# In the expert gather, gelu and weighing take two picks at a time, all but the last four

## The chip, the cores and the metric

The kernel runs on one core of a Trainium2 chip. The metric is the device time of one execution in microseconds (us), the median of several runs.

## The reference, cut to what matters

Two transformer blocks on 256 tokens of 1024 channels, in float32. The last part of the second block is a feed-forward layer that looks up single-neuron experts: for every token and each of 8 heads, 16 of 16384 experts are picked by product keys, and each pick costs one row `u` and one row `v` of 1024 numbers.

```
q = x @ w_query; s = q . sub_keys          # per head, two sides of 128 keys
top 16 per side -> 256 sums -> top 16      # best_s, idx
g = softmax(best_s)                        # 16 weights per head
act = gelu(x . u[idx])                     # one dot product per pick
y = sum over picks of g * act * v[idx]
out = x + y
```

## The kernel before

Everything ahead of the lookup (projections, convolution, attention, the recurrent branch) takes the first 590 us and is untouched. The rest is the gather stage. The tokens are two tiles (`t`) of 128, one token on each partition. A "pick" `g` is one expert slot of one tile: 16 (head, tile) pairs of 16 picks, 256 picks in all. For each pick GpSimd (POOL) starts one indirect DMA (`gather`, L2434) that fetches for each of the 128 tokens its own row of 2048 numbers (`u` and `v` side by side, 8 KB), 1.05 MB in all. For the last two picks (`HALVED`) `u` and `v` come by separate half-size gathers (L2443), all `u` before all `v`.

The rows land in a ring of nine buffers, `UV` (in the profile's names `conv_in`, `big`, `row`, `work_two`). Gather `g` waits until the buffer of pick `g - 9` is free.

Each pick then passes four engines' queues, each of them in order:

- VectorE (DVE): `dot_product(g)` multiplies the `u` half with the normed tokens and sums it up to one number per token (L2062).
- ScalarE (ACT): `spread_value(g)` takes the gelu of that number (L1293). It then waits for the weighing and writes a 128x128 diagonal matrix with the weighed numbers into one of twelve places (L1299).
- VectorE: `weigh(g)` multiplies the gelu with the softmax weight and the inverse of the softmax sum (L2072). It stands behind `dot_product(g + 1)` in VectorE's queue (only in the last picks ahead of it).
- TensorE (PE): `add_value(g)` multiplies the diagonal with the `v` half and adds it up in PSUM, two halves of 512 columns, four matmul records a pick (L779). Its end frees the buffer.

The last pick of all (`LAST`, 255) has no diagonal: `last_value` (L2080) adds it on VectorE, and `add_values` (L2091) then adds the sums from PSUM in two halves, each of which is sent out by a DMA of its own.

Beside this, spread over the picks by hand, the next heads are chosen: `choose` on VectorE (L1961 to L2054) in small steps, one after each pick; `choose_exp` on ScalarE with two loads of its function table (L898) at the picks of `exp_at`, all of them odd numbers. In each quarter of 64 picks the next queries are projected: a weight piece is split into two parts (`hi` on ScalarE, L907, at the first and eighteenth pick; `lo` on VectorE), PE does one group of matmuls after each add of picks 4 to 17 and 22 to 35, ScalarE copies the queries (L1275) at pick 36 of the quarter, PE scores them (L765) at pick 37, ScalarE copies the scores (L1264) at pick 38, and `choose` starts on them. The order inside each engine's queue is the order of the loop over `g`:

```
for g in range(ALL_PICKS):        # DVE
    if g < LAST and g != LAST - 3:
        dot_product(g + 1)
    weigh(g)
    if g == LAST - 3:
        dot_product(g + 1)
    ...                           # one step of choose, lo
```

Of the kernel before, what the change touches and what calls it, by code (L numbers as in the profile page):

```python
# [11 lines left out]
ALU = mybir.AluOpType  # L12
ACT = mybir.ActivationFunctionType
# [27 lines left out]
PEER_TOPK = 16  # L41
# [21 lines left out]
class Marks:  # L63
# [13 lines left out]
    def mark(self, kind, key=None, *others, by=1):  # L77

        value = self.values[kind] = self.values.get(kind, 0) + by
        for name in (("#" + kind, value), (kind, key), *others):  # L80
            self.names[name] = kind, value
        return self.sem(kind), by
# [108 lines left out]
def build(nc, known, x, mem, vectors, weights, rg_w_a, rg_w_x, norm_ffn, sub_keys_t, experts,  # L191
          out):
    with ExitStack() as ctx:
        def sb(name, shape, dt=F32, space=ctx):
            return space.enter_context(nc.sbuf_tensor(name, [P, *shape], dt))

        def psum(name, n):
# [3 lines left out]
        mark, now, at = marks.mark, marks.now, marks.at  # L201
# [13 lines left out]
        probs = Ring("probs", [sb(f"probs{i}", [2, 384]) for i in range(2)])  # L215
        probs_t = Ring("probs_t", [early_small[:, 640 + i * 512:1152 + i * 512] for i in range(2)])
        ident, ones, ones64, later = (sb(n, [P]) for n in (
            "ident", "ones", "ones64", "later"))
# [24 lines left out]
        def tiles4(ap):  # L243
            return ap.rearrange("p (j t) -> p j t", j=4)
# [83 lines left out]
        weight = [sel[:, 256 + t * 128:256 + (t + 1) * 128] for t in range(TT)]  # L328
        dot = [sel[:, 512 + t * 128:512 + (t + 1) * 128] for t in range(TT)]
        coef = dot  # L330
# [42 lines left out]
        for p in range(PIECES_ALL):  # L373
# [15 lines left out]
        diag_places = [probs.buffers[i % 2][:, i // 2 % 2, i // 4 * P:(i // 4 + 1) * P]  # L389
                       for i in range(12)]  # L390
        heads = [(t, h) for i in range(4) for t in range(TT) for h in (2 * i, 2 * i + 1)]
        picks = [(t, h * PEER_TOPK + j) for t, h in heads for j in range(PEER_TOPK)]
# [6 lines left out]
        HALVED = (ALL_PICKS - 2, ALL_PICKS - 1)  # L399
        LAST = ALL_PICKS - 1  # L400
        final_sum = {t: max(g for g in range(LAST) if picks[g][0] == t) for t in range(TT)}
        half_rows = experts.rearrange("n (h d) -> (n h) d", h=2)
        queries, queries_free = tiles4(work_one[:, :]), ("work free", work.holder[1])

# [3 lines left out]
        def under(g):  # L408

            i = g // GROUP + 1  # L410
            return (i, g % GROUP) if i < 4 else (None, None)
# [480 lines left out]
        def act(e):  # L892
            W = Reached(at)
            held = [None]

            def table(*sets):
                if held[0] not in sets:
                    e.preload_act_table_set(sets[0])  # L898
                    held[0] = sets[0]
# [385 lines left out]
                             accum_out=total[t][:, h:h + 1]).then_inc(*mark("pick_exps", head))  # L1285

            def spread_value(g):
                t, n = picks[g]
                here = coef[t][:, n:n + 1]
                table(GELU_TANH)  # L1290
                for wait in W(("dot", g)):
                    e.wait_ge(*wait)
                e.activation(here, here, ACT.Gelu_apprx_tanh).then_inc(*mark("gelu", g))  # L1293
                if g == LAST:
                    return
                for wait in W(("coef", g), ("added", g - 12) if g >= 12 else
                              ("probs free", f"x{2 + g % 2}")):
                    e.wait_ge(*wait)
                e.activation(diag_places[g % 12], ident[:, :], ACT.Copy, scale=here).then_inc(  # L1299
                    *mark("diag", g))  # L1300

            e.dma_start(vec, vectors).then_inc(*mark("load_vec", None, ("loaded", "vec"),
                                                           by=16))
# [18 lines left out]
            for s in slots[:4]:  # L1322
                ahead(s)
                if s.name[:2] == "ub":
                    i = int(s.name[2])
                    table(EXP_TANH)
                    for wait in W(("slot", s.name), work.free(f"th{i}")):
                        e.wait_ge(*wait)
                    e.activation(work.ap(f"th{i}")[:, :], units.ap(s.name)[:, :], ACT.Tanh,
                                 scale=0.5).then_inc(  # L1330
# [6 lines left out]
            for n, s in enumerate(attention):  # L1337
# [15 lines left out]
                elif name[0] == "v":  # L1353
                    i = int(name[1])
                    values_copy(name, v_tm[:, :, i * SLOT:(i + 1) * SLOT])
                elif name[:2] == "xv":
                    i = int(name[2])
                    values_copy(name, xv_tm[:, :, i * SLOT:(i + 1) * SLOT])
                else:
                    i = int(name[1])  # L1360
# [39 lines left out]
            for wait in W(("sums", "mean"), work.free("mean")):  # L1400
                e.wait_ge(*wait)
            e.activation(work.ap("mean")[:, 0:T], units.ap("mean")[:, 0:T], ACT.Copy,
                         scale=1.0 / D).then_inc(*mark("mean", None, ("unit free", "mean")))
# [10 lines left out]
            for wait in W(("sums", "variance"), work.free("rs")):  # L1414
                e.wait_ge(*wait)
            e.activation(rs, units.ap("variance")[:, 0:T], ACT.Ln, bias=EPS5,
                         scale=1.0 / D).then_inc(*mark("ln", "rs", ("unit free", "variance")))
# [40 lines left out]
            for wait in W(("sum", "b2")):  # L1458
                e.wait_ge(*wait)
            e.activation(inv_rms["b2"][1], inv_rms["b2"][1], ACT.Sqrt, bias=EPS6,  # L1460
                         scale=1.0 / D).then_inc(*mark("root", "b2"))
            for wait in W(("inverse", "b2"), ("squares", "b2")):
                e.wait_ge(*wait)
            for t in range(TT):
                a = e.activation(b2_scales[:, t * P:(t + 1) * P], ident[:, :], ACT.Copy,
                                 scale=inv_rms["b2"][1][:, t:t + 1])
# [51 lines left out]
            for t in range(TT):  # L1518
                a = e.activation(v2_tm[:, t, :], tm(units.ap("v2"))[:, t, :], ACT.Copy,
                                 scale=inv_rms["b2"][1][:, t:t + 1])  # L1520
# [36 lines left out]
            for g in range(ALL_PICKS):  # L1557
                spread_value(g)
                if g in exp_at:
                    choose_exp(exp_at[g])  # L1560
                i, at_pick = under(g)
                if i and i > 1 and at_pick == 1:
                    hi(piece(f"pq{i}", 0))
                if i and at_pick == 18:
                    hi(piece(f"pq{i}", 1))
                if i and at_pick == 36:
                    queries_copy(i)
                if i and at_pick == 38:
                    score_copies(i)
                for t in range(TT):  # L1570
                    if g == min(final_pick[t] + 7, ALL_PICKS - 1):
                        for wait in W(("y_out", (t, 1))):
                            e.wait_ge(*wait)
                        e.dma_start(out_tm[:, t, SLOT:D], x_res[:, t, SLOT:D]).then_inc(
                            *mark(f"out{t}1", by=16))
# [3 lines left out]
        def dve(e):  # L1579
            W = Reached(at)  # L1580
# [483 lines left out]
                    op1=ALU.add, accum_out=dot[t][:, n:n + 1]).then_inc(*mark("dot", g))  # L2064

            def weigh(g):
                t, n = picks[g]
                h = n // PEER_TOPK
                here = coef[t][:, n:n + 1]
                for wait in W(("gelu", g), ("chosen", g // PEER_TOPK)):  # L2070
                    e.wait_ge(*wait)
                e.scalar_tensor_tensor(out=here, in0=here, scalar=total[t][:, h:h + 1],  # L2072
                                       in1=weight[t][:, n:n + 1], op0=ALU.mult,
                                       op1=ALU.mult).then_inc(*mark("coef", g))

            def last_value():
# [39 lines left out]
            for wait in W(("lam_exps", None)):  # L2116
                e.wait_ge(*wait)
            e.scalar_tensor_tensor(out=LAM, in0=lam_dots[:, 0:1], scalar=LAMBDA_INIT,
                                   in1=lam_dots[:, 1:2], op0=ALU.add, op1=ALU.subtract).then_inc(
# [21 lines left out]
            for n in (15, 13, 11, 9, 7, 5, 3, 1):  # L2141
                e.wait_ge(*at(now("rg_step"))[1:])
                e.scalar_tensor_tensor(out=rg_acc, in0=rg_acc, scalar=1.0 / n,
                                       in1=rg_z if n == 1 else rg_z2, op0=ALU.add,
# [11 lines left out]
            for s in slots[:4]:  # L2156
                ahead(s)
                if s.name[:2] == "ub":
                    i = int(s.name[2])
                    for wait in W(("tanh", s.name), ("slot", f"ua{i}"), ("const", None)):  # L2160
# [4 lines left out]
                        in1=tiles4(units.ap(f"ua{i}")[:, :]), op0=ALU.add, op1=ALU.mult).then_inc(  # L2165
# [55 lines left out]
            for k in range(KT):  # L2221
                part = conv_acc[:, k, :]
                for wait in W(("root", "rs")):
                    e.wait_ge(*wait)
                e.scalar_tensor_tensor(out=part, in0=part, scalar=v("conv_ln_g", k), in1=rs,
                                       op0=ALU.mult, op1=ALU.mult).then_inc(
# [3 lines left out]
            for half in range(2):  # L2230
                part = half_of(conv_acc, half)
                for wait in W(("tanh", f"z{half}")):
                    e.wait_ge(*wait)
                e.scalar_tensor_tensor(out=part, in0=tiles4(work.ap(f"z{half}")[:, :]), scalar=1.0,
                                       in1=part, op0=ALU.add, op1=ALU.mult).then_inc(
# [21 lines left out]
            for i in range(2):  # L2257
# [4 lines left out]
                for t in range(TT):  # L2262
                    s = e.scalar_tensor_tensor(
                        out=part[:, t, :], in0=unit[:, t * SLOT:(t + 1) * SLOT], scalar=0.5,
                        in1=part[:, t, :], op0=ALU.mult, op1=ALU.add)
# [22 lines left out]
            for k in range(RG_WIDTH):  # L2288
                for j in range(RG_TILES):
# [8 lines left out]
                    else:  # L2298
                        s = e.scalar_tensor_tensor(out=xc[:, j, :], in0=src, scalar=tap,
                                                   in1=xc[:, j, :], op0=ALU.mult, op1=ALU.add)  # L2300
# [69 lines left out]
            for g in range(ALL_PICKS):  # L2370
                if g in choose_at:
                    steps = choose(choose_at[g])
# [5 lines that stand above are left out]
                if g == final_pick[0] + 4:  # L2378
                    add_values(0)
                i, at_pick = under(g)  # L2380
                if g == 8:
                    normed_tile(1)
                if i and i > 1 and at_pick == 3:
                    lo(piece(f"pq{i}", 0))
                if i and at_pick == 19:
                    lo(piece(f"pq{i}", 1))
                for _ in range(2 if 4 <= g < 8 else 1):
                    next(steps, None)
# [194 lines left out]
```

## Time and profile before

| what | value |
|---|---|
| median of 3 runs | 1237.87 us (1237.71 to 1238.59) |
| the profiled execution | 1239.19 us |
| its span, first to last instruction | 1237.0 us |
| TensorE busy | 1097.0 us (89%) |
| VectorE busy | 979.1 us (79%) |
| ScalarE busy | 549.7 us (44%) |
| GpSimd busy | 590.0 us (48%) |
| moved by DMA | 374.23 MB |
| mean granted TensorE clock | 0.989 |

The busy times are of the whole span. The profiled execution has its own time, a little above the median; a sum made from its rows is compared with that time.

### The profile page before, as it was taken

Reading aid. Unit: us, or ns where it says so; the run is one execution under the profiler, and the core shown is the slowest. Engines: PE = TensorE matmul, PEld = TensorE weight load, DVE = VectorE, ACT = ScalarE, POOL = GpSimd, SP = SyncE. Lnnn points to the kernel's source line nnn. Section 1 sums busy time; section 2 is a strip of 40 time slices with the busy share of each in tenths; the row PEclk is TensorE's granted clock in tenths of the full one; section 3 lists DMA queues with packets and bytes.
Section 4 is the critical chain, followed back from the end, with each engine's and each line's share of the span. In section 5 each row is a group of like instructions: output and inputs, shape, how many; then the busy total and the mean of one; then the engine's idle time right before and its main releaser. Section 6 shows DMA issues by size and latency. Waiting matters only on the chain.

```text
span 1237.0 us, 13575 instructions
## 1 busy us (share of the span) xinstructions
PE 1097.0 (89%) x4676; PEld 724.1 (59%) x4676; DVE 979.1 (79%) x1960; ACT 549.7 (44%) x1070; POOL 590.0 (48%) x547
## 2 busy tenths in 40 slices
PE   6999999999999999999588887888879888787877
PEld 6988888788989889977244433444324443222322
DVE  6599999998887767686988777887778867877655
ACT  5665676654456444994433233323332233222311
POOL 0089999999840000010554545553545545444432
PEclk9999999999999999999799999999999999999999
DMA  6554434444464655336899999999999999999996
GB/s 248 193 182 170 171 137 139 155 149 165 176 214 160 225 188 179 132 137 255 358 427 426 428 427 428 426 427 426 426 427 427 427 427 427 427 427 410 427 427 275
DMA packets 53941, 374.23 MB, mean 303 GB/s; under 512 B 6896, under 2 KB 6896, under 8 KB 9200
## 3 DMA queue, kind: packets, MB, share of 16 engines
q0 software_dynamic: 37152, 268.45, 51.6%
q1 hardware_dynamic: 14512, 100.67, 22.8%
q10 hardware_dynamic: 2208, 4.24, 1.0%
q8 instruction: 37, 0.61, 0.2%
q14 instruction: 32, 0.26, 0.1%
HBM read 372.29 MB, written 1.05 MB: 302 GB/s over the span
## 4 chain that ended last, share of the span: by engine, by line
PE 44%; DMA 25%; DVE 24%; ACT 4%; issue 3%; POOL 0%; POOLq 0%; DVEq 0%; SPq 0%; ACTq 0%
DMA big<-in_experts,big 11%; PE unit L450 10%; PE unit L452 10%; PE unit L451 10%; PE unit L779 9%; DMA row<-in_experts,big 6%; DMA conv_in<-in_experts,big 4%; DVE w_lo L1589 3%; DVE row L2062 3%; DMA work_two<-in_experts,big 2%; DVE big L2062 2%; DVE big L1968 2%; DVE conv_acc L1612 2%; DVE big L1965 2%; DVE big L2072 1%
## 5 line engine op out<-in xcount | busy, mean ns | idle before, releaser
L1299 ACT ACTIVATE probs<-ident,big 128x128 f32<-128x128 f32 x255 | 102.4, 402 | 430.8 <-DVE big L2072 430.8
L779 PE MATMUL unit<-row,probs 128*128 128x512 f32 x448 | 215.4, 610 | 45.9 <-ACT probs L1299 45.7
L1589 DVE TENSOR_TENSOR w_lo<-w_raw,w_hi 128x2048 fp32r<-128x2048 f32 x89 | 207.6, 2339 | 50.3 <-ACT w_hi L907 50.3
L907 ACT CAST w_hi<-w_raw 128x2048 fp32r<-128x2048 f32 x89 | 169.4, 1905 | 87.3 <-DMA w_raw<-in_weights 45.8
L779 PE MATMUL unit<-big,probs 128*128 128x512 f32 x344 | 168.3, 620 | 39.3 <-ACT probs L1299 39.2
L2434 POOL DMA_INDIRECT row<-in_experts,big x112 | 134.2, 1198 | 128.6 <-PE unit L779 112.1
L450 PE MATMUL unit<-in_hi,w_hi 128*128 128x256 f32 x544 | 189.2, 348 | 1.6 <-DVE in_lo L1676 0.9
L450 PE MATMUL unit<-w_hi,in_hi 128*128 128x512 f32 x432 | 171.0, 396 | 0.7 <-ACT big L1044 0.7
L779 PEld LDWEIGHTS unit<-row,probs 128*128 128x128 f32 x448 | 78.3, 190 | 156.1 <-ACT probs L1299 97.2
L451 PE MATMUL unit<-w_hi,in_lo 128*128 128x512 f32 x432 | 168.3, 390 | 0.0
L452 PE MATMUL unit<-w_lo,in_hi 128*128 128x512 f32 x432 | 168.3, 390 | 0.0
L2062 DVE CUSTOM_DVE_ANT_0 row<-big,row 128x1024 f32<-128x1024 f32 x112 | 136.6, 1220 | 37.7 <-DMA row<-in_experts,big 37.6
L2434 POOL DMA_INDIRECT big<-in_experts,big x85 | 102.7, 1208 | 118.3 <-PE unit L779 104.3
L451 PE MATMUL unit<-in_lo,w_hi 128*128 128x256 f32 x544 | 153.7, 283 | 0.0
L452 PE MATMUL unit<-in_hi,w_lo 128*128 128x256 f32 x544 | 153.6, 282 | 0.0
L2415 POOL TENSOR_TENSOR conv_acc<-conv_acc,big 128x256 f32<-128x256 f32 x132 | 140.6, 1065 | 11.0
L2411 POOL TENSOR_SCALAR big<-conv_in,early_small 128x256 f32<-128x256 f32 x132 | 136.6, 1035 | 3.5 <-DVE conv_acc L1612 2.5
L779 PEld LDWEIGHTS unit<-big,probs 128*128 128x128 f32 x344 | 61.3, 194 | 127.7 <-ACT probs L1299 80.2
L2062 DVE CUSTOM_DVE_ANT_0 big<-big 128x1024 f32<-128x1024 f32 x87 | 106.1, 1219 | 34.3 <-DMA big<-in_experts,big 34.3
L450 PEld LDWEIGHTS unit<-in_hi,w_hi 128*128 128x128 f32 x544 | 104.2, 191 | 23.0 <-issue 20.5
L451 PEld LDWEIGHTS unit<-in_lo,w_hi 128*128 128x128 f32 x544 | 104.1, 191 | 20.5 <-issue 20.3
L452 PEld LDWEIGHTS unit<-in_hi,w_lo 128*128 128x128 f32 x544 | 104.0, 191 | 0.0
(319 smaller groups left out, 1672.0 us busy)
## 6 DMA issues: line engine op xcount, KB each, us to landing
w_raw<-in_weights SPq DMA_DIRECT2D x90, 1024.0 KB, 4.8
w_waiting<-in_weights SPq DMA_DIRECT2D x2, 1024.0 KB, 9.1
row<-in_experts,big POOLq DMA_INDIRECT x112, 14.8
big<-in_experts,big POOLq DMA_INDIRECT x89, 13.4
big<-in_x SPq DMA_DIRECT2D x2, 512.0 KB, 5.1
big<-in_mem ACTq DMA_DIRECT2D x1, 1024.0 KB, 4.9
big<-in_x ACTq DMA_DIRECT2D x1, 1024.0 KB, 6.6
big<-in_sub_keys_t ACTq DMA_DIRECT2D x1, 1024.0 KB, 6.8
```

The source lines that it names most:

```text
L450: e.matmul(unit[:, to], *hi_hi, start=first, stop=False)
L451: e.matmul(unit[:, to], *hi_lo, start=False, stop=False)
L452: m = e.matmul(unit[:, to], *lo_hi, start=False, stop=final)
L779: m = e.matmul(unit[:, half * 512:(half + 1) * 512], diag_places[g % 12], UV.ap(g)[:, D + half * 512:D + (half + 1) * 512], start=first, s ...
L907: e.copy(split.ap(p)[0][:, :, :], raw.ap(p)[:, :, :]).then_inc(*mark("hi", p))
L1299: e.activation(diag_places[g % 12], ident[:, :], ACT.Copy, scale=here).then_inc(*mark("diag", g))
L1589: e.tensor_tensor(lo_part[:, :, :], raw.ap(p)[:, :, :], hi_part[:, :, :].bitcast(F32), ALU.subtract).then_inc(*mark("lo", p))
L1612: i = e.scalar_tensor_tensor(out=dst, in0=src, scalar=tap, in1=dst, op0=ALU.mult, op1=ALU.add)
L2062: e.tensor_tensor_reduce(out=row_u, in0=h3[:, t, :], in1=row_u, scale=1.0, scalar=0.0, op0=ALU.mult, op1=ALU.add, accum_out=dot[t][:, n:n ...
L2411: e.tensor_scalar(product, src, tap, 1.0, ALU.mult, ALU.mult).then_inc(*mark("pool_product", (t, k)))
L2415: e.tensor_tensor(dst, dst, product, ALU.add).then_inc(*mark("pool_tap", None, *done))
L2434: e.indirect_dma_start(out=UV.ap(g), out_offset=None, in_=experts, in_offset=bass.IndirectOffsetOnAxis(ap=expert[t][:, n:n + 1], axis=0)). ...
```

## The change

`together(g)` says which picks are dealt with at step `g`: none at an even `g`, `g - 1` and `g` at an odd one, and from pick 252 (`PAIRED`) on each by itself. `spread_value` and `weigh` use it: one gelu and one weighing take two columns of the same head, at the odd pick, behind the dot product of the odd one (gelu) and of the next (weighing). The two diagonals stay two instructions, one behind the other. Dot products, adds and gathers are as they were.

```diff
+        PAIRED = LAST - 3
+
+        def together(g):
+
+            return range(g, g + 1) if g >= PAIRED else range(g - 1, g + 1) if g % 2 else range(0)
...
             def spread_value(g):
-                t, n = picks[g]
-                here = coef[t][:, n:n + 1]
+                if not together(g):
+                    return
+                t, n = picks[together(g)[0]]
+                some = coef[t][:, n:n + len(together(g))]
                 table(GELU_TANH)
                 for wait in W(("dot", g)):
                     e.wait_ge(*wait)
-                e.activation(here, here, ACT.Gelu_apprx_tanh).then_inc(*mark("gelu", g))
+                e.activation(some, some, ACT.Gelu_apprx_tanh).then_inc(*mark("gelu", g))
                 if g == LAST:
                     return
-                for wait in W(("coef", g), ("added", g - 12) if g >= 12 else
-                              ("probs free", f"x{2 + g % 2}")):
-                    e.wait_ge(*wait)
-                e.activation(diag_places[g % 12], ident[:, :], ACT.Copy, scale=here).then_inc(
-                    *mark("diag", g))
+                for i, pick in enumerate(together(g)):
+                    for wait in W(("coef", g), ("added", pick - 12) if pick >= 12 else
+                                  ("probs free", f"x{2 + pick % 2}")):
+                        e.wait_ge(*wait)
+                    e.activation(diag_places[pick % 12], ident[:, :], ACT.Copy,
+                                 scale=some[:, i:i + 1]).then_inc(*mark("diag", pick))
...
             def weigh(g):
-                t, n = picks[g]
-                h = n // PEER_TOPK
-                here = coef[t][:, n:n + 1]
+                if not together(g):
+                    return
+                t, n = picks[together(g)[0]]
+                h, end = n // PEER_TOPK, n + len(together(g))
+                here = coef[t][:, n:end]
                 for wait in W(("gelu", g), ("chosen", g // PEER_TOPK)):
                     e.wait_ge(*wait)
                 e.scalar_tensor_tensor(out=here, in0=here, scalar=total[t][:, h:h + 1],
-                                       in1=weight[t][:, n:n + 1], op0=ALU.mult,
+                                       in1=weight[t][:, n:end], op0=ALU.mult,
                                        op1=ALU.mult).then_inc(*mark("coef", g))
```

## Rows read from the trace of the kernel before

**Rows 1.** The page: TensorE's busy time, DMA share in 40 slices, the gathers' queue.

```profile
PE 1097.0 (89%) x4676; PEld 724.1 (59%) x4676; DVE 979.1 (79%) x1960; ACT 549.7 (44%) x1070; POOL 590.0 (48%) x547
...
DMA  6554434444464655336899999999999999999996
...
q0 software_dynamic: 37152, 268.45, 51.6%
```

**Rows 2.** Stretches of the gather stage: length, busy per engine, granted clock, DMA share, GB/s.

```profile
590.00:595.00 5.00, 1.33 (x10) 0.97 (x8) 4.54 (x22) 3.52 (x4) 3.78 (x5) 0.83 0.70 236
...
600.00:700.00 100.00, 86.08 (x268) 43.35 (x268) 82.45 (x247) 33.08 (x96) 49.96 (x41) 0.97 1.01 427
...
1118.80:1122.00 3.20, 3.17 (x4) 1.43 (x5) 2.67 (x8) 0.74 (x4) 0.00 (x0) 0.52 1.02 433
...
1125.00:1130.00 5.00, 4.38 (x11) 1.63 (x9) 2.61 (x6) 0.49 (x2) 3.43 (x3) 1.00 0.97 382
```

**Rows 3.** The same columns for two microseconds near the end.

```profile
1224.00:1225.00 1.00, 1.00 (x3) 0.38 (x2) 0.74 (x1) 0.00 (x0) 0.00 (x0) 1.00 0.54 221
...
1230.00:1231.00 1.00, 1.00 (x3) 0.50 (x4) 0.61 (x3) 0.36 (x2) 0.00 (x0) 1.00 0.06 25
```

**Rows 4.** The chain that ended last, its last three long pieces: start, length, what.

```profile
1219.26 12.40 DMA big<-in_experts,big
...
1231.76 1.29 DVE big L2080
...
1233.15 0.69 DVE big L2091
```

**Rows 5.** Gelu and weighing, grouped by line: busy, mean ns | idle before, releaser.

```profile
L2072 DVE SCALAR_TENSOR_TENSOR big<-big 128x1 f32<-128x1 f32 x256 | 55.4, 216 | 31.7 <-ACT big L1293 31.7
L1293 ACT ACTIVATE big<-big 128x1 f32<-128x1 f32 x256 | 48.2, 188 | 3.9 <-DVE big L2062 3.7
```

**Rows 6.** Waits of VectorE from 590 us on: total, times, longest.

```profile
DVE big L2072 <- ACT big L1293: 31.7, 23, 2.2
```

**Rows 7.** The timeline of all engines near the end: start, length, instruction, idle before.

```profile
1223.66 1.98 PE L779 MATMUL unit<-row,probs 128*128 128x512 f32 x4 [0.46 <-ACT probs L1299]
...
1224.26 1.23 DVE L2062 CUSTOM_DVE_ANT_0 conv_in<-big,conv_in 128x1024 f32<-128x1024 f32 x1 [1.09 <-DMA conv_in<-in_experts,big]
...
1225.41 0.22 DVE L2072 SCALAR_TENSOR_TENSOR big<-big 128x1 f32<-128x1 f32 x1
1225.66 0.40 ACT L1299 ACTIVATE probs<-ident,big 128x128 f32<-128x128 f32 x1 [1.96 <-DVE big L2072]
...
1226.12 1.98 PE L779 MATMUL unit<-work_two,probs 128*128 128x512 f32 x4 [0.47 <-ACT probs L1299]
...
1229.82 3.70 PE L779 MATMUL unit<-big,probs 128*128 128x512 f32 x8
```

**Rows 8.** Timelines by engine: POOL's issues, the first add, the first quarter's switch.

```profile
588.92 1.93 POOL L2434 DMA_INDIRECT conv_in<-in_experts,big  x1 [27.08 <-DVE big L2034]
...
601.82 3.78 PE L779 MATMUL unit<-conv_in,probs 128*128 128x512 f32 x4 [9.81 <-ACT probs L1299]
...
668.89 1.44 POOL L2434 DMA_INDIRECT row<-in_experts,big  x1 [1.48 <-PE unit L779]
...
692.14 1.07 ACT L1275 COPY work_one<-unit 128x512 f32<-128x512 f32 x2 [2.22 <-PE unit L452]
...
695.88 1.95 PE L765 MATMUL bank<-big,work_one 128*128 128x128 f32 x16
...
697.76 0.29 DVE L1965 MAX8 big<-conv_acc 128x8 f32<-128x128 f32 x1 [2.92 <-ACT conv_acc L1264]
...
699.48 1.21 DVE L2062 CUSTOM_DVE_ANT_0 row<-big,row 128x1024 f32<-128x1024 f32 x1
699.82 1.68 POOL L2434 DMA_INDIRECT big<-in_experts,big  x1 [2.57 <-PE unit L779]
```

**Rows 9.** The chain that ended last, its piece for pick 55: issue to landing.

```profile
719.21 13.55 DMA big<-in_experts,big
```

## The prediction

> **What bounds the kernel now.** I read the page first. TensorE (PE) is busy for 89% of the span, but the DMA line stands at 9 from slice 19 to the end, and one queue, that of the gathers, moves 268.45 MB of the 374 [rows 1]. So the last 640 us are one stage, and it has to be judged by itself. The stretches of that stage come next [rows 2]: between 590 and 595 us the DMA engines start to move rows (236 GB/s over 5 us is 1.18 MB, at 427 GB/s 2.8 us of work, so data flows from about 592.2 on); from 600 on they are fully busy at 427 GB/s. VectorE (DVE) has 82 of 100 us there, ScalarE (ACT) 33, PE 86. 256 picks of 1.05 MB at 427 GB/s are 2.456 us each, 629 us in all, and 592.2 + 629 = 1221. The only dent shown, at 1125 to 1130, is 382 GB/s.
>
> The end is to be looked at closer [rows 3]. In 1224 to 1225 the DMA share is 0.54, but in 1230 to 1231 it is still 0.06, which is one engine of sixteen. One DMA engine runs some 5.5 us behind the other fifteen, and a row has landed only when the last engine is done. The chain says the same [rows 4]: it goes through the last transfer, landed at 1219.26 + 12.40 = 1231.66, then the last value on DVE (L2080), then the two halves of L2091, and ends. Nothing an engine does ahead of a landing is on the path, as long as a gather is always waiting in the queue.
>
> **What is removed.** Picks 0 to 251 become 126 pairs, so 126 of 256 gelus and 126 of 256 weighings go. A gelu takes 188 ns, so ACT has 23.7 us less; a weighing takes 216 ns [rows 5]. The instruction behind a weighing starts 0.14 us after it (in the timeline below, the DVE row after one), so DVE gets about 126 x 0.14 = 17.6 us back. The DVE also waits 31.7 us in all, in 23 stalls, for a gelu [rows 6]; most are gelus held up behind table loads or casts, and a pair's gelu has a pick more of time, so I expect most of these to go. All of this, up to 49 us of DVE, lies beside transfers that take 2.456 us a pick whatever DVE does: I cost it at nothing. Were the DMA cover gone, it would be worth those tens of us.
>
> The Trainium skill ("VectorE: DVE Perf Modes", the section on the TRN2 errata) says that an SBUF-source operation pays a fixed latency per instruction, so that merging small ones saves nearly a whole one each. By that rule VectorE gains the 17.6 us and more; it only turns into time if VectorE is the bound, which is a rival below.
>
> **What is moved.** In steady state the order for one pick is [rows 7]: dot product 1224.26, weighing 1225.41, diagonal (L1299) 1225.66, the four matmuls of the add 1226.12 for 1.98 us. With pairs the even pick's coefficient comes one dot product later, 2.45 us; the odd one's coefficient is at its old time, but its add stands behind the even one's, 1.72 us later (eight matmuls take 3.70, four 1.98). A row's buffer is freed by its add, and the gather nine picks on waits for that. No DMA is added or reordered; each is issued 1.7 to 2.45 us later.
>
> What covers this is the queue. Pick 55 was issued at 719.21 and landed at 732.76 [rows 9]; issue takes 0.94, its own transfer 2.46, so it stood ready for about 10 us. The least that works is the first gather's: issued by 588.92 + 1.93 = 590.85 [rows 8], flowing at about 592.2, so 1.35 us. Two places are thinner. Pick 33: counted back from pick 55 it lands at 732.76 - 22 x 2.456 = 678.7 and starts at 676.3; its issue ended at 668.89 + 1.44 = 670.33. That is 5.9, less 1.35 leaves 4.6, less a step of 2.45 leaves 2.1 us.
>
> The other is each quarter's switch (picks 38, 102 and 166; I work out the first). ACT copies the queries at 692.14 [rows 8] once PE has finished pick 35's share; the pair of 36 and 37 has both gelu and diagonals behind that. The score matmuls (695.88) come after the add of 37 and so find two adds ahead of them where there was one: 1.72 later. Queued behind their wait are ACT's score copies, then DVE's choosing (L1965, 697.76, already stalled), then dot 40 (699.48, now about 701.2). The pair of 38 and 39 is weighed only after that dot, at 702.4; the add of 38 runs 703.1 to 705.1, and gather 47, issued at 699.82, goes to about 705.3, 5.4 later. Pick 47 starts to move at 732.76 - 9 x 2.456 = 710.7; issue ended at 701.5, so 9.2 less 1.35 is 7.8 us, and 2.4 remain. Gain side: DVE is early by 0.14 a pair and by the stalls gone, up to a few us; I take none. So the cost of the moved adds is bounded by 0 and by what is missing if 2.4 is wrong; I take 0.
>
> **The clock.** The granted clock was 0.52 between 1118.8 and 1122.0 [rows 2], after PE had been idle about 1.9 us. At the lower level (1.2 GHz) four matmuls took 3.78 us [rows 8], against 1.98. Steady gaps on PE are 0.46 us a pick now (2.44 less 1.98); pairs make them 4.9 - 3.7 = 1.2 us, and at a quarter's switch about 3.5 us (699.6 to 703.1). The Trainium skill ("TensorE: Matmul & The Clock Gate", Part 1) has it that idle gaps between bursts bring the lower level back, which speaks against this change. The trace agrees that it can happen after a gap; it does not happen at most gaps. By the row an occasional half-clock add costs 1.8 us of the queue's reserve and no time; by the rule each quarter's switch would pay it, and that is the rival below.
>
> **The tail.** The last four picks stay single, but the pair 250 and 251 stands just ahead. Today 250 is added at 1223.66 and 251 at 1226.12, after its weighing at 1225.41 [rows 7]. With the change both are weighed at 1225.41, so PE starts at 1226.12 as now, with one add more to do: 250, 251, 252, 253, 254 in a row. Five adds without a break are 1.98 + 4 x 1.72 = 8.86: end at 1234.98, first half of the last one at 1234.12. Today the last two end at 1229.82 + 3.70 = 1233.52, under cover of L2080, which ends at 1233.05; L2091's two halves start at 1233.15 and 1233.79 [rows 4, 7]. With the change they start at 1234.2 and 1235.05. That is +1.25 us on the output. Lower bound 0 (PE fits its adds in, if the diagonal of 250 were early), upper bound 1.8 (a lower clock for one add) + 1.25 = 3. I take 1.25 because each term has a row.
>
> **Sum.** 0 (removed) + 0 (moved) + 1.25 (tail). The profiled execution took 1239.19 us for a span of 1237.0, 1.3 above the median; part of that is the dent at 1125. 1239.19 + 1.25 = 1240.4 for it, and 1237.87 + 1.25 = 1239.1 us for the median. What a measurement can tell from no change is about 0.2%, 2.5 us.
>
> **Rivals.** (a) The tail is hidden: DVE or a landing is later than PE after all. For it: the margin is one add. Against it: five adds at 1.72. 1237.9 us.
> (b) The queue runs dry at the quarter switches. Place: gathers 47, 111, 175 and those just behind. With 2.4 us left and 1.8 lost for each add at the lower clock, it decides from the second half-clock add on: 2 x 1.8 - 2.4 = 1.2 short, at three places 3.6, and the tail's 1.25: 1242.7. For it: the gap of 3.5 us. Against it: even where the queue was thinnest (pick 33) the rate was 427 GB/s, and later the slowest engine has 5.5 us more in hand than the others.
> (c) VectorE was the bound at least in part, and the 17.6 us count: for it only its 82%; against it, the flat 427 GB/s. Some 1220 us.
> (d) The change does what it says but nothing is late: that is (a).
>
> **How the numbers follow.** Forecast 0.62, (a) 0.22, (b) 0.12, (c) 0.04. The first two are within 0.2%, with a little of the forecast's upper bound (3 us) beyond it. Faster 0.03, same 0.85, slower 0.12. The range takes in (a) with the spread of the runs, and most of the way to (b): 1237.2 to 1241.6.
>
> **What the new profile would show.** Right: 130 gelus and 130 weighings; DMA at 427 GB/s through the stage; the wait of the weighing for a gelu mostly gone; PE in bursts of eight matmuls; and at the end one burst of twenty matmuls from about 5.6 us before the last landing, with a gap of about 1.1 us between L2080's end and the final halves, and PE in the chain there. Wrong: windows under 420 GB/s just after a quarter's switch (b), a final half that still starts 0.1 us after the last value (a), or a stage that is shorter from first to last gather (c). What I can't see from here is how the sixteen engines drift against each other when gathers come in pairs.

## The result and the profile after

The changed kernel takes 1245.6 us (median; 1243.02 to 1245.97), the kernel before beside it 1238.23 (1237.71 to 1238.67): a ratio of 1.0055 [1.0043, 1.0067], some 6.8 us slower. A second series gave 1243.23 against 1237.78, 1.0047 [1.0034, 1.0061], 5.8 us (one execution of the kernel before took 6191.61 us in that series, which leaves the median where it is). The forecast of 1239.1 was wrong and the measured time lies above its range (up to 1241.6), in the direction of rival (b). The profiled execution took 1243.02 us for a span of 1240.8 and is the shortest of the first series, so its trace shows only part of the loss: 3.8 us against the profiled execution before.

VectorE and ScalarE have less to do, TensorE and GpSimd have as many instructions as before, and the queue of the gathers moves the same bytes. These lines of the page answer to [rows 1]:

```profile
PE 1090.0 (88%) x4676; PEld 730.7 (59%) x4676; DVE 959.9 (77%) x1834; ACT 535.1 (43%) x944; POOL 569.3 (46%) x547
...
DMA  7444443434554555345999999999999999999997
...
q0 software_dynamic: 37152, 268.45, 51.8%
...
L1301 ACT ACTIVATE big<-big 128x2 f32<-128x2 f32 (+1 forms) x130 | 26.4, 203 | 185.6 <-DVE big L2071 185.4
```

1960 - 1834 = 126 instructions are gone from VectorE and as many from ScalarE, and 130 gelus are left. The waits of VectorE, from 588 us to the end, answer to [rows 6]; the columns are total, times, longest:

```profile
DVE big L2083 <- ACT big L1301: 15.2, 9, 3.8
DVE big L1974 <- ACT conv_acc L1270: 14.3, 3, 4.8
```

The weighing waits half as long as before (15.2 for 31.7). But the choosing now waits up to 4.8 us for the copies of the scores, where the stall was 2.92 [rows 8]. That wait exists three times, once behind each quarter's switch, and there the stream of rows breaks. The stretches have the columns of [rows 2]:

```profile
600.00:700.00 100.00, 84.71 (x264) 43.55 (x264) 76.45 (x214) 29.30 (x72) 45.36 (x40) 0.95 1.01 423
...
704.00:707.00 3.00, 3.00 (x4) 1.04 (x4) 2.93 (x9) 0.20 (x1) 0.00 (x0) 0.50 1.00 423
707.00:710.00 3.00, 3.00 (x5) 1.22 (x4) 2.86 (x12) 0.69 (x2) 0.94 (x1) 0.55 0.57 191
710.00:715.00 5.00, 5.00 (x13) 2.10 (x12) 4.93 (x15) 1.10 (x4) 3.34 (x3) 1.00 0.90 321
...
864.00:868.00 4.00, 4.00 (x7) 1.70 (x7) 3.93 (x12) 0.48 (x2) 0.61 (x1) 0.66 1.02 426
868.00:872.00 4.00, 4.00 (x10) 1.53 (x9) 3.79 (x16) 0.62 (x3) 1.29 (x2) 1.00 0.90 330
...
1025.00:1028.00 3.00, 3.00 (x6) 1.36 (x5) 3.00 (x9) 0.20 (x1) 0.16 (x1) 0.65 1.01 429
1028.00:1032.00 4.00, 4.00 (x10) 1.74 (x10) 3.83 (x17) 0.90 (x3) 2.45 (x3) 1.00 0.88 324
...
1100.00:1200.00 100.00, 74.78 (x163) 29.08 (x162) 67.97 (x171) 23.87 (x68) 43.71 (x40) 1.00 1.01 427
...
1233.00:1234.00 1.00, 1.00 (x4) 0.39 (x3) 0.44 (x4) 0.49 (x2) 0.00 (x0) 1.00 0.06 25
```

The same thing happens three times: first a lower granted clock (0.50 to 0.66 in these stretches), then a rate far below 427 GB/s. At the first switch 3 us at 191 and 5 us at 321 are 1.66 + 1.24 = 2.9 us of missed transfer, counted as the time that the missing bytes would take at 427 GB/s. In the last quarter, where no queries are projected, pairs are as frequent as anywhere and the rate is 427.

How it comes about at the first switch is seen in the order of TensorE's work (start, length, engine, line, and in brackets the idle time ahead and its releaser):

```profile
692.20 0.28 PE L457 MATMUL unit<-in_lo,w_hi 128*128 128x256 f32 x1
692.32 0.28 PE L458 MATMUL unit<-in_hi,w_lo 128*128 128x256 f32 x1
694.55 1.98 PE L785 MATMUL unit<-conv_in,probs 128*128 128x512 f32 x4 [1.96 <-ACT probs L1308]
696.37 1.88 PE L785 MATMUL unit<-big,probs 128*128 128x512 f32 x4
698.09 1.95 PE L771 MATMUL bank<-big,work_one 128*128 128x128 f32 x16
703.53 6.75 PE L785 MATMUL unit<-big,probs 128*128 128x512 f32 x8 [3.50 <-ACT probs L1308]
```

and in those of ScalarE, VectorE and GpSimd:

```profile
692.63 1.07 ACT L1281 COPY work_one<-unit 128x512 f32<-128x512 f32 x2 [4.40 <-PE unit L458]
693.59 0.22 ACT L1301 ACTIVATE big<-big 128x2 f32<-128x2 f32 x1
694.10 0.69 ACT L1308 ACTIVATE probs<-ident,big 128x128 f32<-128x128 f32 x2 [0.29 <-DVE big L2083]
...
699.97 0.30 DVE L1974 MAX8 big<-conv_acc 128x8 f32<-128x128 f32 x1 [4.76 <-ACT conv_acc L1270]
...
701.70 1.21 DVE L2071 CUSTOM_DVE_ANT_0 row<-big,row 128x1024 f32<-128x1024 f32 x1
...
698.52 0.94 POOL L2445 DMA_INDIRECT big<-in_experts,big  x1 [0.78 <-PE unit L785]
707.59 0.94 POOL L2445 DMA_INDIRECT big<-in_experts,big  x1 [8.13 <-PE unit L785]
711.05 0.94 POOL L2445 DMA_INDIRECT big<-in_experts,big  x1 [2.53 <-PE unit L785]
```

Pick 36 is even, so its gelu and diagonal no longer stand ahead of the copy of the queries. ScalarE waits at that copy until TensorE has finished pick 35's matmuls, and TensorE then waits 1.96 us for the diagonal of 36, which stands behind the copy. Scores, choosing and dot product 40 follow late; the pair 38 and 39 is weighed only after that dot product; TensorE has been idle for 3.50 us, runs its eight matmuls at the lower clock (6.75 us instead of 3.70), and gather 47 is started at 707.59. GpSimd had waited 8.13 us for that.

The end, in the chain of waits (start, length, what):

```profile
1213.22 13.64 DMA conv_in<-in_experts,big
...
1228.28 0.41 ACT probs L1308
...
1228.74 8.87 PE unit L785 x20
...
1237.63 0.69 DVE big L2102
```

and the last value in the timeline:

```profile
1234.38 1.28 DVE L2091 SCALAR_TENSOR_TENSOR big<-big 128x1024 f32<-128x1024 f32 x1 [0.36 <-DMA big<-in_experts,big]
```

From the start of the last value to the second final half it was 1233.79 - 1231.76 = 2.03 us [rows 4, 7]; now it is 1237.63 - 1234.38 = 3.25, 1.22 more. The twenty matmuls have taken the place of the last transfer in the chain.

### The profile page after: what moved, and what is told of

Read it like the earlier page. It is cut to its first block, busy times and chain, and to the rows that moved or that the text cites. A ratio compares the mean times of both kernels' runs of the same rounds, so it can differ in the third digit from the quotient of the medians.

```text
span 1240.8 us, 13202 instructions
## 1 busy us (share of the span) xinstructions
PE 1090.0 (88%) x4676; PEld 730.7 (59%) x4676; DVE 959.9 (77%) x1834; ACT 535.1 (43%) x944; POOL 569.3 (46%) x547
## 3 DMA queue, kind: packets, MB, share of 16 engines
HBM read 372.29 MB, written 1.05 MB: 301 GB/s over the span
## 4 chain that ended last, share of the span: by engine, by line
PE 47%; DVE 25%; DMA 21%; ACT 4%; issue 3%; POOL 0%; SPq 0%; DVEq 0%; ACTq 0%; POOLq 0%
DMA big<-in_experts,big 16%; PE unit L785 11%; PE unit L456 10%; PE unit L458 10%; PE unit L457 10%; DVE big L2071 4%; DVE w_lo L1598 3%; DVE row L2071 3%; DVE big L1977 2%; DMA conv_in<-in_experts,big 2%; DMA work_two<-in_experts,big 2%; DVE big L1974 2%; DVE conv_acc L1621 2%; ACT probs L1308 1%; DVE conv_acc L1970 1%
## 5 line engine op out<-in xcount | busy, mean ns | idle before, releaser
L785 PE MATMUL unit<-row,probs 128*128 128x512 f32 x448 | 211.5, 606 | 45.5 <-ACT probs L1308 45.4
L1308 ACT ACTIVATE probs<-ident,big 128x128 f32<-128x128 f32 x255 | 88.6, 394 | 238.8 <-DVE big L2083 238.8
L2445 POOL DMA_INDIRECT row<-in_experts,big x112 | 123.9, 1106 | 139.7 <-PE unit L785 130.2
L2445 POOL DMA_INDIRECT big<-in_experts,big x85 | 92.8, 1091 | 126.3 <-PE unit L785 117.8
L2426 POOL TENSOR_TENSOR conv_acc<-conv_acc,big 128x256 f32<-128x256 f32 x132 | 143.3, 1085 | 11.0
L785 PEld LDWEIGHTS unit<-big,probs 128*128 128x128 f32 x344 | 65.1, 200 | 129.0 <-issue 65.0
L1301 ACT ACTIVATE big<-big 128x2 f32<-128x2 f32 (+1 forms) x130 | 26.4, 203 | 185.6 <-DVE big L2071 185.4
```

What stands on the lines that cost most here:

```text
L785: m = e.matmul(unit[:, half * 512:(half + 1) * 512], diag_places[g % 12], UV.ap(g)[:, D + half * 512:D + (half + 1) * 512], start=first, s ...
L1301: e.activation(some, some, ACT.Gelu_apprx_tanh).then_inc(*mark("gelu", g))
L1308: e.activation(diag_places[pick % 12], ident[:, :], ACT.Copy, scale=some[:, i:i + 1]).then_inc(*mark("diag", pick))
L2426: e.tensor_tensor(dst, dst, product, ALU.add).then_inc(*mark("pool_tap", None, *done))
L2445: e.indirect_dma_start(out=UV.ap(g), out_offset=None, in_=experts, in_offset=bass.IndirectOffsetOnAxis(ap=expert[t][:, n:n + 1], axis=0)). ...
```

## The experiments

All were timed beside the kernel before, in three series in which it had 1238.55, 1237.78 and 1238.07 us; kernels of different series are compared by their ratios to it. Line numbers shift by up to three in some of them. The first three divide the change by place; the theory was that the loss lies at the quarter switches and in the tail, the rival that it lies in the pairs as such.

**Single picks at the switches** (`e1_single_at_switch`):

```diff
-            return range(g, g + 1) if g >= PAIRED else range(g - 1, g + 1) if g % 2 else range(0)
+            if g >= PAIRED or g < 192 and g % GROUP in (36, 37, 38, 39):
+                return range(g, g + 1)
+            return range(g - 1, g + 1) if g % 2 else range(0)
```

> The changed kernel, but picks 36 to 39 of the first three quarters are dealt with singly. Theory A (the queue of gathers runs dry just behind each quarter's switch, because the adds of 38 and 39 come late there and at the lower clock): the DMA rate stays above 420 GB/s in the stretches behind the switches, gathers 47, 111 and 175 are issued some 5 to 7 us earlier against their neighbours, and of the 7.4 us lost some 5 come back: about 1240.5 us. Theory B (every pair costs a little everywhere, since each gather is issued a step later): 12 picks of 256 less, at most 0.4 us back: about 1245.

Measured: 1240.14 against 1238.55, 1.0010 [1.0001, 1.0019]. Six pairs out of 126, and most of the loss is gone; the 1.2 us left are less than the tail costs by the runs below. The stretches behind the first switch:

```profile
707.00:710.00 3.00, 3.00 (x6) 1.16 (x5) 2.87 (x11) 0.20 (x1) 0.48 (x1) 0.64 1.01 429
710.00:715.00 5.00, 4.97 (x11) 2.01 (x10) 4.97 (x15) 1.22 (x5) 2.71 (x3) 0.88 1.01 428
```

The clock was down for a while here too (0.64), but nothing was missed.

**Single picks ahead of the tail** (`e2_tail_single`): `PAIRED = LAST - 5` for `LAST - 3`, so 250 and 251 are single.

> The changed kernel with picks 250 and 251 single too. Theory A (the five adds in a row end 1.2 us after the last value): the last burst on PE is 16 matmuls, the two final halves start 0.1 and 0.7 us after L2091's end, and 1.2 us come back: about 1244.4 us. Theory B (the last landing sets the end and PE is hidden): 1245.6.

Measured: 1242.36, 1.0034 [1.0021, 1.0048]; against the two series of the changed kernel 1.6 and 2.6 us come back, with intervals that overlap. The chain ends as before the change, at the landing, and the dent behind the switch stays (238 GB/s from 707 to 710):

```profile
1224.91 9.96 DMA big<-in_experts,big
...
1234.96 1.30 DVE big L2091
...
1236.35 0.69 DVE big L2102
```

**Pairs at the switches alone** (`e3_pairs_only_at_switch`): as the first, with the condition turned round: `if not (g < 192 and g % GROUP in (36, 37, 38, 39))`, and no `PAIRED`.

> The reverse of e1: all picks single but 36 to 39 of the first three quarters, 6 pairs in all. Theory A: the loss behind each switch is there, the tail is as before the change: 1238.2 plus 3 to 5, about 1242. Theory B (a little for each pair): 6 of 126 pairs, 0.4 us: 1238.6.

Measured: 1240.19, 1.0015 [1.0006, 1.0024], about half of what was expected. The dents are there (336 GB/s from 707 to 710, 356 from 710 to 715), but smaller, and the stretch from 665 to 675, which has 388 and 383 GB/s in the changed kernel, is at 427. The loss at the switches is therefore more than these pairs by themselves cost; it takes the pairs around them too.

**TensorE kept busy over the gap** (`e4_pe_kept_busy`): seven extra multiplications behind the scores, whose result nothing uses, on TensorE where it would idle.

```diff
+                    for _ in range(7):
+                        e.matmul(units.buffers[2][:, 0:256], ident[:, :], h3[:, 0, 0:256],
+                                 start=True, stop=True)
```

> The changed kernel with seven extra matmuls of 128x256 (result unused) on PE behind the scores of pick 37, where PE now waits about 3.5 us; they take about 3.0 us. Nothing else differs. If the lower clock is what empties the queue (each add 1.8 us longer): no stretch at 0.5 behind the three switches, gather 47 is issued 1.8 us sooner and 48 3.5 us, and most of the loss there goes: about 1241.5. If the late adds alone do it and the clock adds nothing: 1245.6, or a little more for the extra work.

Measured: 1242.6 (1239.92 to 1243.88), 1.0031 [1.0018, 1.0043]; the trace is of the shortest execution. In it the gap of 3.50 us is 0.47, the clock stays, and gather 47 goes 1.6 us sooner:

```profile
700.03 3.19 PE L896 MATMUL unit<-big,ident 128*128 128x256 f32 x14
703.69 3.70 PE L785 MATMUL unit<-big,probs 128*128 128x512 f32 x8 [0.47 <-ACT probs L1311]
...
705.95 0.94 POOL L2448 DMA_INDIRECT big<-in_experts,big  x1 [6.33 <-PE unit L785]
```

```profile
704.00:707.00 3.00, 3.00 (x8) 1.14 (x6) 2.93 (x9) 0.20 (x1) 0.94 (x1) 1.00 1.01 429
707.00:710.00 3.00, 2.14 (x5) 0.87 (x5) 2.86 (x11) 0.69 (x2) 0.94 (x1) 1.00 0.99 393
```

By ratios against the two series of the changed kernel, 0.0016 to 0.0024, 2 to 3 us, come back, although the intervals touch or overlap. So the clock is a part of the loss, as far as so small a difference can show, and not all of it: with it held here, 0.0031 of 1238, 3.8 us, remain, more than the tail's 1.25.

**ScalarE's work moved behind the pair** (`e5_act_after_pair`, `e10_cast_after_pair`, `e11_copy_after_pair`). If what is late is the pair's gelu and diagonals behind ScalarE's other work, it is enough to let that work come one pick later and to keep all the pairs. The second `hi` cast goes from pick 18 of a quarter to 19, the copy of the queries from 36 to 37:

```diff
-                if i and at_pick == 18:
+                if i and at_pick == 19:
...
-                if i and at_pick == 36:
+                if i and at_pick == 37:
```

Both edits:

> The changed kernel, pairs as they are, but ScalarE's two pieces of quarter work that stand between the picks of a pair are put behind the pair: the cast of the second weight piece from pick 18 to pick 19, the copy of the queries from pick 36 to pick 37. Theory A1 (a good part of the lateness comes from gelus and diagonals that wait behind work which itself waits for TensorE): the 6.8 us at the lower clock around 647 us go or shrink, the scores of the first switch start some 1.8 us sooner, gather 47 too, and about 2 to 3 of the 7 us lost come back: about 1242.5. Theory A2 (only the pairing of 38 and 39 counts, which waits for the scores in any case): 1245, as the changed kernel.

The cast alone:

> The changed kernel with only the cast of the second weight piece put from pick 18 to pick 19. The changed kernel is 5.4 us above the one before: 1.25 the tail, 4.1 the queue. If the late adds of the first quarter's picks 18 to 26 carry over into its switch, this brings back a good part, 2 us: 1241.2. If only the switch counts: 1243.2.

The copy alone:

> The changed kernel with only the copy of the queries put from pick 36 to pick 37. If the wait of the pair of 36 and 37 for it, and the lower clock that follows, make up the loss at the three switches: 2.5 to 3.5 us come back, 1240. If the cast at pick 18 carries more of it: 1242 or more.

Measured: both, 1239.32, 1.0013 [1.0004, 1.0022]; the cast alone, 1244.22, 1.0049 [1.0035, 1.0063]; the copy alone, 1239.61, 1.0014 [1.0004, 1.0023]. So the cast does nothing and the copy everything: 0.0049 - 0.0014 = 0.0035 of 1238, 4.3 us, by the two kernels of one series (against the two series of the changed kernel itself it is 4.1 and 5.1). In the trace with the copy alone, the diagonals now stand ahead of the copy and TensorE runs from group to scores without a gap:

```profile
691.93 0.70 ACT L1308 ACTIVATE probs<-ident,big 128x128 f32<-128x128 f32 x2 [2.38 <-DVE big L2083]
...
693.17 1.07 ACT L1281 COPY work_one<-unit 128x512 f32<-128x512 f32 x2 [0.54 <-PE unit L458]
```

```profile
696.40 1.95 PE L771 MATMUL bank<-big,work_one 128*128 128x128 f32 x16
701.84 6.72 PE L785 MATMUL unit<-big,probs 128*128 128x512 f32 x8 [3.49 <-ACT probs L1308]
```

The gap of 3.49 us and the lower clock behind it are still there in this execution (1241.12 us, its longest), and 710 to 715 has 323 GB/s. With both edits the profiled execution (1239.46) shows the same gap, but not the lower clock, and 426 to 429 GB/s in the three stretches from 704 to 715:

```profile
701.77 3.70 PE L785 MATMUL unit<-big,probs 128*128 128x512 f32 x8 [3.49 <-ACT probs L1308]
...
704.02 0.94 POOL L2445 DMA_INDIRECT big<-in_experts,big  x1 [6.33 <-PE unit L785]
```

**The changed kernel once more** (`after_again`), to have its time beside these:

> The changed kernel once more, on the same chip as the others. Expected 1245, with a wider spread than the kernel before (its four runs were 1243.0 to 1246.0), since how many adds fall on the lower clock differs from run to run.

Measured: 1243.23 (1242.26 to 1244.84), 1.0047. Here the eight matmuls took 5.40 us, gather 47 went at 706.87, and 707 to 710 has 262 GB/s.

**A ring of eight buffers under the kernel before** (`e6_before_8_buffers`): each gather waits for the buffer of pick `g - 8`, one step of lateness everywhere, with no pairs.

```diff
-                *rows[2:], *rows[:2], work_two[:, :]]
+                *rows[2:], *rows[:2]]
```

> The kernel before, no pairs, with eight row buffers in place of nine: every gather waits for the add of the pick eight before and so is issued one pick, 2.46 us, later, about what pairing does to it outside the switches. If lateness of one step is itself the cost, all through the stage (theory B): some 1242 or more. If the reserve of the queue covers one step and only the extra waits and the lower clock of the pairs empty it (theory A): no stretch under 400 GB/s behind the switches, 1238.6 to 1239.6.

Measured: 1238.84, 1.0011 [1.0001, 1.0020]; behind the switch 423 to 431 GB/s. A whole pick of reserve less, 2.46 us everywhere, costs about 1 us and opens no dent at the switch. The change's lateness there is well over one pick: gather 47 is issued at 707.59 for 699.82 [rows 8], 7.8 us later.

**Single wherever a pair was late** (`e7_single_where_late`): single at picks 18, 19 and 36 to 39 of the first three quarters and from 250 on. **Both remedies together** (`e9_act_after_pair_tail_single`): all pairs up to 249, with cast and copy moved.

> The changed kernel with singles at picks 18, 19 and 36 to 39 of the first three quarters and from pick 250 on; 107 pairs are left. Theory A (the loss sits at these places and the tail, the other pairs are free): the kernel before, 1238.6 us within 0.6. Theory B (pairs cost a little everywhere): 1238.6 plus 107/126 of what is then left of the loss, 1240 or more.

> e5 (both pieces of ScalarE's work behind the pair) with picks 250 and 251 single: 125 pairs. e5 was 1.5 us above the kernel before, which I take for the tail. Then this one is the kernel before, 1237.8 within 0.5. If something of the switches is left in e5, and the tail is less than 1.5: 1238.5 or more.

Measured: 1237.69, 0.9998 [0.9989, 1.0008], and 1238.34, 1.0000 [0.9991, 1.0009]. 116 pairs in the first (125 less 9; the 107 of the expectation is a miscount) and 125 in the second cost nothing, and they gain nothing.

The second does so although its trace still has the gap, the lower clock and the dents at the first switch. A dent by itself need not cost time:

```profile
701.10 6.48 PE L785 MATMUL unit<-big,probs 128*128 128x512 f32 x8 [3.50 <-ACT probs L1308]
```

```profile
707.00:710.00 3.00, 3.00 (x9) 1.33 (x8) 2.90 (x11) 0.20 (x1) 1.34 (x2) 1.00 0.96 377
710.00:715.00 5.00, 4.93 (x12) 2.00 (x11) 5.00 (x12) 1.60 (x5) 3.60 (x3) 1.00 0.92 305
```

**The pair 250 and 251 alone** (`e8_pair_only_in_tail`), all others single:

> The kernel before with one single pair, picks 250 and 251. By the working of the prediction the adds of 250 to 254 run in one burst of 8.86 us and the two halves of the output start 1.1 and 1.25 us later: 1239.0, 1.2 us above the kernel before. If the last landing hides it: 1237.8.

Measured: 1240.53 (1238.7 to 1240.74), 1.0017 [1.0008, 1.0026]. One pair costs 2.1 us by the ratio. The eleven executions fall into two groups, three of 1238.7 to 1239.19 us and eight of 1240.52 to 1240.74; what divides them was not found, and the trace is of the shortest. In it the chain ends like that of the changed kernel:

```profile
1224.44 8.87 PE unit L787 x20
...
1233.33 0.69 DVE big L2104
```

## Why the prediction was wrong, step by step

**What bounds the kernel:** right. VectorE and ScalarE have less to do, and the time follows the gathers. Bytes and rate outside the dents are unchanged.

**What is removed costs nothing and gives nothing:** right, counts and all (126 and 126). The wait of the weighing for a gelu fell to 15.2 us, half, not "most". The busy time fell by 19.2 us on VectorE, for 17.6 forecast, but by only 14.6 on ScalarE, for 23.7. No kernel of the series beats the kernel before; rival (c) is out, by the two runs at 0.9998 and 1.0000.

**What is moved costs nothing:** this is the step that failed, namely "I take 0" with "2.4 remain" at gather 47. Its path was right. Forecast and found are: scores 697.6 and 698.09, dot product 40 701.2 and 701.70, the add of 38 703.1 and 703.53. They are 0.4 to 0.5 us apart, which is the copy's 692.63 for 692.14. Two terms were wrong:

- The start that pick 47 needs. It was counted back from the landing of pick 55, which is that of the slowest DMA engine, the one that at the end ran 5.5 us behind the others [rows 3]. Counted from the front, 592.2 + 47 x 2.456 = 707.6, not 710.7. The runs agree: with the end of its issue at 704.96 (cast and copy moved) nothing was missed, at 706.89 (TensorE kept busy) 393 GB/s in 3 us are 0.24 us missed, at 708.53 (changed) 1.66. By 707 us the gathers had moved 48.77 MB before, 48.87 in the changed kernel and 48.80 with TensorE kept busy, so the need was the same there; with cast and copy moved it was 48.27, 1.2 us more time. Against 706.25, which is 707.6 less the 1.35 from issue to flow, gather 47 would have been just on time at 705.3 + 0.94, with nothing left of the 2.4 us. Pick 33, the other thin place, was counted back in the same way. From the front it had 592.2 + 33 x 2.456 - 1.35 - 670.33 = 1.6 us to spare, less than the step of 2.45 taken off it. In the changed trace its issue ends only 0.1 us later (669.38 + 1.05), and still the rate from 665 to 675 is 388 and 383 GB/s, 0.96 us missed.
- The clock. "An occasional half-clock add costs reserve and no time" had no reserve to draw on. Of the 2.3 us by which gather 47 (707.59) is later than forecast, 0.4 to 0.5 are the shift just named, and the rest is the add of 38 at the lower clock; the add of 39 then puts gather 48 at 711.05. The Trainium skill ("TensorE: Matmul & The Clock Gate", Part 1), that gaps between bursts bring the lower level back, is borne out at all three switches in the changed kernel, and the forecast gave it too little weight; but it isn't a law of this gap, as the run at 3.70 us shows.

The 1.96 us that TensorE idled ahead of the add of 36 was not named in the prediction, though it had the pair of 36 and 37 behind the copy. It is the same lateness, seen one step sooner. The experiment with the copy alone shows that this order is what costs: 4.3 us of the 5.8 to 6.8, the lower clock included, which has 2 to 3 of them by the run with TensorE kept busy.

**The tail, +1.25:** right in its mechanism and in the trace (+1.22, and a burst of 8.87 us for 8.86). By ratios the tail costs 2.1 us alone and 0.0013 of 1238, 1.6 us, between the two runs with the copy moved, so the forecast value is at the low side of what was measured.

**Rival (b):** place and sign right, 1242.7 us worked out, 1243.23 and 1245.6 measured; its chance of 0.12 was too small. Against it stood that "the slowest engine has 5.5 us more in hand than the others". That is rather a loan: the other fifteen engines may fall some 5 us back before the last landing moves. The trace shows it being used up. Missed transfer in the changed profile is 2.9 us at the first switch and, from 330 and 324 GB/s in 4 us, 0.9 and 1.0 in the first stretches behind the others, 4.8 in these alone. But the last value starts only 2.6 us later (1234.38 for 1231.76), while the stage began 1.2 us earlier in its span (342 GB/s from 590 to 595 for 236).

All fourteen traces bear the loan out; ten of them are here. Columns: what the gathers moved up to 640 us and from 640 to 1200, in MB; the start of the last value; the transfer missed against 238.04 MB, at 427 GB/s; and the length of the stage, from 640 us less the time of the first column's bytes at 427 GB/s to the last value.

| kernel | to 640 | 640 to 1200 | last value | missed, us | stage, us |
|---|---|---|---|---|---|
| `e8_pair_only_in_tail` | 20.82 | 238.04 | 1230.09 | 0.0 | 638.8 |
| before | 20.22 | 237.69 | 1231.76 | 0.8 | 639.1 |
| `e7_single_where_late` | 20.65 | 237.19 | 1229.94 | 2.0 | 638.3 |
| `e9_act_after_pair_tail_single` | 20.69 | 236.37 | 1230.94 | 3.9 | 639.4 |
| `e4_pe_kept_busy` | 20.69 | 235.94 | 1231.27 | 4.9 | 639.7 |
| `e11_copy_after_pair` | 20.78 | 235.59 | 1232.49 | 5.7 | 641.2 |
| `e3_pairs_only_at_switch` | 20.10 | 235.40 | 1233.56 | 6.2 | 640.6 |
| `after_again` | 20.75 | 234.78 | 1233.65 | 7.6 | 642.2 |
| changed | 20.71 | 234.22 | 1234.38 | 9.0 | 642.9 |
| `e10_cast_after_pair` | 20.75 | 233.80 | 1235.59 | 9.9 | 644.2 |

Up to 4.9 us missed, the stage is as long as without (638.3 to 639.7); from 5.7 on it grows by about what is missed more. So a first dent is nearly free and the next ones cost their full size, and the parts don't add up: 1.9 us for the pairs at the switches alone, whose 6.2 us missed lie mostly within the loan, but 4.3 back when only the copy is moved, which takes 9.9 down to 5.7. No run was made to try the loan by itself, and a row of the table is one execution.

## What to carry to other kernels

A batch of two moves the first member's work one step back in every in-order queue, past whatever stood between the two; look for an instruction in between that waits for another engine (here a copy waiting for TensorE), and let the batch go first. Where a stream of transfers is the bound, count the reserve of a refill from the front of the stream, not back from a landing, which is that of the slowest DMA engine. A saving on engines that the bound hides is worth nothing, so any lateness that it brings can only lose: nothing as long as the reserve covers it (ratios of 0.9998 and 1.0000 with 116 and 125 pairs), all of it past that, and at the end of the stage, where no reserve is left, at once.

## What the runs showed of the hardware that had not been expected

- The same idle time of TensorE ahead of the same eight matmuls gave either level of its clock: 3.70 us of work after 3.49 us in one kernel, 6.72 after 3.49 in another, 5.19 after 3.49 in a third (`e3_pairs_only_at_switch`) and 6.75 after 3.50 in the changed one. It isn't the order of the work: `e9_act_after_pair_tail_single` has the same order at this place as the first of these (`e5_act_after_pair`) and took 6.48 us after 3.50. A shorter gap can do it too: with the cast alone moved, the two adds behind 1.96 us of idle time took 2.90 and 2.70 us, for 1.98 and 1.88 in the changed kernel behind the same gap. In all of them the sixteen score matmuls (1.95 us) stand ahead of the gap. The changed kernel's times spread over 1242.26 to 1245.97 us in its two series, which would fit that; it was not shown to be the reason.
- One DMA engine of sixteen ends behind the rest (a share of 0.06 in the last microsecond). Missed transfer first shows as the others ending nearer to it: in the changed kernel the share is still 0.63 from 1231 to 1232, 2.3 us ahead of the last landing, while before it was 0.54 from 1224 to 1225, 6.7 us ahead of it [rows 3].

```profile
1231.00:1232.00 1.00, 1.00 (x4) 0.52 (x3) 1.00 (x4) 0.00 (x1) 0.00 (x0) 1.00 0.63 258
```
